# Four layers in one launch: one shared weight buffer whose next layer's weights are loaded before the layer before it ends, and the modulation's products made on DVE inside the second layer

## The reference, cut to what matters

```python
def first_block(x, positions, ...):
    for layer in range(DEPTH):                  # DEPTH = 2
        if layer % 2 == 0:
            x = _even_layer(x, *even_params[layer // 2])     # x @ w_in (3088 wide), gated linear attention, spatial gating
        else:
            x = _odd_layer(x, positions, *odd_params[layer // 2])   # x @ w_in (2560 wide), rotary, retention, pooling
    return x

def second_block(x, c, w_ada, b_ada, g_pre, w_in, ...):
    mod = jax.nn.silu(c) @ w_ada[layer] + b_ada[layer]       # [1024] @ [1024, 3072]
    shift, scale, gate = jnp.split(mod, 3, axis=-1)
    h = rmsnorm(x, g_pre[layer]) * (1.0 + scale[:, None, :]) + shift[:, None, :]
    proj = h @ w_in[layer]                                   # 3792 + 64 columns, split over the last two layers
    o_a = gated_deltanet(...)                                # third layer of the kernel
    o_b = dsa_sparse_attention(...)                          # fourth layer of the kernel
    mix = jnp.concatenate([o_a, o_b], axis=-1) @ w_out[layer]
    return x + gate[:, None, :] * rmsnorm(mix, g_post[layer])
```

## Time and profile before

| what | us |
|---|---|
| median of 3 runs (4527.81 to 4532.61) | 4531.23 |
| the profiled execution | 4529.71 |
| its span, first to last instruction | 4527.8 |
| PE busy | 4082.2 |
| DVE, ACT, POOL busy | 1905.7, 1396.9, 790.8 |
| mean granted clock of PE | 0.963 |

### The profile page before, as it was taken

One profiled execution on the slowest core, in us unless ns is written; L12 is line 12 of the kernel. 1 busy time (PEld: TensorE's weight loads), 2 busy tenths in 40 slices (PEclk: granted clock), 3 DMA queues, 4 the chain that ended last, 5 costly groups with the idle time before them and its releaser, 6 DMA issues. The chain is left out here.

```text
span 4527.8 us, 57307 instructions
## 1 busy us (share of the span) xinstructions
PE 4082.2 (90%) x23038; PEld 2629.7 (58%) x23038; DVE 1905.7 (42%) x4316; ACT 1396.9 (31%) x2956; POOL 790.8 (17%) x548
## 2 busy tenths in 40 slices
PE   7999999996799999996899999997789989898877
PEld 4555555553355555553688888886665656555544
DVE  0111111212122222222255555654046687688875
ACT  1222222222111111111133333332144445455552
POOL 1223323323022222221122222221000000000000
PEclk9999999998899999998999999996899999999998
DMA  5000000000400000003400000000310000000000
GB/s 180 19 14 14 19 19 9 19 19 10 168 19 19 19 19 19 19 19 104 154 23 25 25 25 25 20 15 6 136 33 33 22 29 17 31 20 17 17 12 17
DMA packets 73482, 161.03 MB, mean 36 GB/s; under 512 B 18053, under 2 KB 32058, under 8 KB 72250
## 3 DMA queue, kind: packets, MB, share of 16 engines
q1 hardware_dynamic: 73274, 158.14, 9.9%
HBM read 120.37 MB, written 37.75 MB: 35 GB/s over the span
## 5 line engine op out<-in xcount | busy, mean ns | idle before, releaser
L287 PE MATMUL e_ps<-e_w_in,e_xT 128*128 128x440 f32 (+1 forms) x1792 | 688.0, 538 | 1.8 <-DMA e_w_in<-l_w_in 1.8
L772 PE MATMUL o_ps<-o_w_in,o_xT 128*128 128x512 f32 x1280 | 565.0, 595 | 11.5 <-ACT o_xT L875 10.6
L287 PEld LDWEIGHTS e_ps<-e_w_in,e_xT 128*128 128x128 f32 x1792 | 332.9, 191 | 303.1 <-issue 295.8
L772 PEld LDWEIGHTS o_ps<-o_w_in,o_xT 128*128 128x128 f32 x1280 | 239.5, 191 | 290.9 <-issue 290.8
L1294 PE MATMUL d_ps<-d_hT,d_w_in 128*128 128x128 f32 x3072 | 392.9, 282 | 13.3 <-ACT d_hT L1485 11.3
L1294 PEld LDWEIGHTS d_ps<-d_hT,d_w_in 128*128 128x128 f32 x3072 | 360.0, 193 | 29.1 <-ACT d_hT L1485 12.7
L2096 PE MATMUL s_ps<-s_hT,s_w_in 128*128 128x128 f32 x2304 | 275.0, 280 | 8.1 <-DMA s_w_in<-w_in 5.6
L2096 PEld LDWEIGHTS s_ps<-s_hT,s_w_in 128*128 128x128 f32 x2304 | 270.9, 197 | 13.2 <-DMA s_w_in<-w_in 6.9
L856 PE MATMUL o_ps<-o_w_out,o_gt 128*128 128x512 f32 x512 | 225.2, 598 | 4.5 <-ACT o_gt L929 4.5
L2220 PE MATMUL s_ps<-s_w_out,s_catT 128*128 128x512 f32 x512 | 227.1, 597 | 0.0
L2238 PE MATMUL s_ps<-s_ikT,s_iqT 64*128 64x512 f32 (+3 forms) x608 | 168.5, 632 | 63.2 <-ACT s_Lg L2358 62.5
(11 more groups left out here) (408 smaller groups left out, 6106.6 us busy)
## 6 DMA issues: line engine op xcount, KB each, us to landing
d_ada<-w_ada SPq DMA_DIRECT2D x8, 1536.0 KB, 6.6
o_w_in<-l_w_in SPq DMA_DIRECT2D x5, 2048.0 KB, 17.8
e_xb<-x SPq DMA_DIRECT2D x16, 512.0 KB, 3.5
x<-e_gl SPq DMA_DIRECT2D x16, 512.0 KB, 2.6
o_xb<-x SPq DMA_DIRECT2D x16, 512.0 KB, 3.2
x<-o_cat SPq DMA_DIRECT2D x16, 512.0 KB, 2.6
d_xb<-x SPq DMA_DIRECT2D x16, 512.0 KB, 3.3
hT<-d_hT SPq DMA_DIRECT2D x16, 512.0 KB
```

The lines of the kernel that those rows point to most:

```text
L287: m = pe.matmul(bank[c % 2][:, 0:n], xT[:, k * P:(k + 1) * P], W_in[:, k, a:a + n], start=(k == 0), stop=(k == KT - 1))
L772: m = pe.matmul(bank[c % 2][:], xT[:, k * P:(k + 1) * P], W_in[:, k, off:off + 512], start=(k == 0), stop=(k == KT - 1))
```

## The change

One tile `arena` (128 partitions, 3088 columns by 8) is allocated once, and every layer's `W_in` is a view of its front. What lies behind a smaller `W_in` holds tables of that layer (`Carve`). `xb` (two blocks of x) and `ident` are shared too. A new class `Ahead` holds a layer's weight parts with their semaphores, so that the layer before it can issue the loads: SP does so as soon as the last block's projections are made (`proj_made.upto(BLOCKS - 1)`). The first two blocks of x, or for the last layer the first block of `hT`, are loaded ahead too. The small tables still load after the barrier.

Each layer's start is written in another order: weights ahead of tables in `even_layer`, PE's waits for `loaded` and `W_out` behind block 0's projections, the positions loaded as 16 rows and turned by PE. The product with `w_ada` leaves `delta_layer`. In each of the 16 blocks of `odd_layer` SP loads 192 columns of `w_ada` (8 rows of 768 bytes a partition, 0.79 MB), DVE multiplies them with `ccol` and adds up each partition's 8 rows, and SP stores the 128 x 192 sums to `mod_parts`. `delta_layer` loads `mod_parts` (1.57 MB) and adds the 128 partitions with six products with `ones`.

```diff
+class Ahead:
+    def __init__(self, sem, name, W_in, weights, parts, rows=None, xb=None):
...
+    def load_weights(self, eng):
+        for part, ready in zip(self.parts, self.w_loaded):
+            for dst, src in part:
+                eng.dma_start(dst, src).then_inc(ready.sem, 16)
+    def weights(self, n):
+        return self.w_loaded[n].sem, 16 * len(self.parts[n])
+    def load_rows(self, eng, n):
+        eng.dma_start(self.xb[:, n, :], self.rows[n * P:(n + 1) * P, :]).then_inc(self.x_in[n].sem, 16)
...
 # even_layer, SP
+            sp.dma_start(ident[:], ident_d).then_inc(ident_loaded.sem, 16)
+            own.load_rows(sp, 0)
+            own.load_weights(sp)
+            own.load_rows(sp, 1)
             with nc.allow_non_contiguous_dma(reason="small tables"):
...
             body(Blk(BLOCKS // 2 - 1, 0), load=False)
+            sp.wait_ge(stored.sem, 16 * (BLOCKS - 1) + 1)
+            ahead.load_rows(sp, 0)
+            sp.wait_ge(*proj_made.upto(BLOCKS - 1))
+            ahead.load_weights(sp)
+            sp.wait_ge(*r_ready.upto(BLOCKS - 1))
+            ahead.load_rows(sp, 1)
             body(Blk(BLOCKS // 2 - 1, 1), load=False)
...
 # odd_layer, SP
             def body(b, load=True):
+                sp.wait_ge(*ada_made.before(b.i))
+                sp.dma_start(ada, ada_v[:, :, bass.ds(b.i * ADA_N, ADA_N)]).then_inc(ada_in.sem, 16)
...
+                sp.wait_ge(*ada_made.upto(b.i))
+                sp.dma_start(mod_parts[:, bass.ds(b.i * ADA_N, ADA_N)], ada_sum[:]).then_inc(ada_stored.sem, 16)
                 sp.wait_ge(*out_ready.upto(b.i))
...
             body(Blk(BLOCKS // 2 - 1, 0), load=False)
+            sp.wait_ge(*proj_made.upto(BLOCKS - 1))
+            ahead.load_weights(sp)
             body(Blk(BLOCKS // 2 - 1, 1), load=False)
...
 # odd_layer, DVE, in each block
                 dve.tensor_tensor(cat[:, 0:512], cat[:, 0:512], gates[:, p, 0:512], ALU.mult).then_inc(*oc_ready.inc())
+                dve.wait_ge(ada_in.sem, 16 * i + 16)
+                dve.tensor_tensor(ada, ada, spread(ccol[:], ADA_N), ALU.mult).then_inc(*o.inc())
+                o.settle()
+                dve.wait_ge(ada_stored.sem, 16 * i + 1)
+                dve.tensor_reduce(ada_sum[:], ada.rearrange("p k n -> p n k"), AX.X, ALU.add).then_inc(*ada_made.inc())
                 dve.wait_ge(*y_made.upto(i))
...
 # delta_layer, SP and PE
-            for k in range(2, KT):
-                sp.wait_ge(ada_used.sem, k - 1)
-                load_ada(k)
-            for (a, n), part in zip(w_parts, w_loaded):
-                sp.dma_start(W_in[:, :, a:a + n], wv[:, :, a:a + n]).then_inc(part.sem, 16)
...
+                if b.i == BLOCKS - 2:
+                    sp.wait_ge(*proj_made.upto(BLOCKS - 1))
+                    sp.wait_ge(h_stored.sem, 16 * BLOCKS + 1)
+                    h_first.load(sp, 0)
+                    ahead.load_weights(sp)
...
-            pe.wait_ge(*c_ready.upto(0))
-            for k in range(KT):
-                pe.wait_ge(aloaded[k % 2].sem, 16 * (k // 2) + 16)
-                for n in range(6):
-                    m = pe.matmul(bank[n][:], cB[:, k, :], ada[:, k % 2, n * 512:(n + 1) * 512], start=(k == 0), stop=(k == KT - 1))
-                m.then_inc(*ada_used.inc())
+            pe.wait_ge(*ones_ready.upto(0))
+            pe.wait_ge(mod_loaded.sem, 16)
+            for n in (2, 3, 0, 1, 4, 5):
+                pe.matmul(bank[n][:], ones[:], mod[:, n * 512:(n + 1) * 512], start=True, stop=True).then_inc(*mod_made.inc())
...
 # sparse_layer, PE: block 0 waits for its weights alone, and the bias table is waited for behind block 1
+            for c in range(4):
+                pe.wait_ge(*own.weights(c))
+                project(0, c)
             pe.wait_ge(loaded.sem, NSMALL)
...
+            transpose_ckv(0)
             for c in range(4):
-                pe.wait_ge(w_loaded[c].sem, 16 * len(w_parts[c]))
-                project(0, c)
+                project(1, c)
+            pe.wait_ge(*cT_ready.upto(0))
             pe.wait_ge(loaded2.sem, 64)
```

338 lines of the change are left out of this document (179 added, 159 removed).

## The result

| | before | after |
|---|---|---|
| median of the runs, us | 4529.52 (4 runs, 4524.45 to 4532.61) | 4426.64 (4 runs, 4423.76 to 4429.24) |
| span of the profiled execution, us | 4527.8 | 4423.8 |
| PE / DVE busy, us | 4082.2 / 1905.7 | 4037.5 / 1977.8 |

The ratio is 0.9774, with a 95% interval of 0.9757 to 0.9791: 103 us faster, where the sum of the forecast was 92. The difference of the two profiled executions, 104.0 us, is read off at the same events in each. A start is counted from DVE's first instruction behind the barrier.

What follows compares the result with a forecast made beforehand. Blocks were taken as PE-bound, with layer starts waiting for loads; -9.0 - 27.9 - 45.8 - 9.5 = -92.2 us from 4529.7 gave 4437.5, stated as 4438 for the median; own range 4430 to 4447, wide range 4424 to 4453.

Steps and rivals of the forecast that it cites:

- three signs of being wrong: Idle PE ended by `conv_w` tables later than 2140, a sum over 4 us, or a wait for weights behind a barrier.
- More is gained: Rival: tables no limit at program start (-14 instead of -9), queue faster at other starts; -100, 4430 us; chance 0.08.
- first condition: At the program's start, tables are no limit, so that start gains 14 us instead of 9.
- Program start, -9.0: First layer's loop waits for tables but no longer for `W_out`, beginning at 53 instead of 62.07 us.
- Second layer, -27.9: Early weights and angles out of the way: first projection at 1133.1, loop at 1164.0 instead of 1191.93 us.
- Third layer, -47.8: `w_ada` product gone, `conv_w` tables late next: first projection at 2144.4 instead of 2192.25 us.
- The +1 for the lower clock in the projection: Third layer's first projection: PE, having stood idle longer, runs a first stretch at lower clock, costing 1 us.
- Tail of the second layer, +1: Block 15's `w_ada` share, queued behind 8.4 MB of weights, delays the end 1 us; 7 at 265 GB/s.
- The products cost nothing: Second layer's DVE product and sum, 3.6 us a block, hide in 17.9 us idle; sum priced 1.83, at most 3.7.
- Fourth layer, -9.5: Earlier first projection, partly lost to block 1's wait for `hT` behind the bias row; block 2 at 3247.7 instead of 3257.15.

Runs made afterwards that it cites:

- angles_first: Changed kernel with the second layer's old starting order restored: positions turned and sine, cosine made before x and the first projection; 4438.42 us.
- late_weights: Changed kernel with the early loads undone: each layer's x rows, turned h and weights issued at its own start; 4460.81 us.
- second pair: Kernel before and changed kernel, each executed and profiled once more without edits; 4534.62 us and 4429.08 us.
- product_back: Changed kernel with the `w_ada` product moved back to the third layer on PE, and its loads and DVE work removed from the second; 4470.15 us.
- tables_split: Changed kernel with the third layer's four `conv_w` loads on their own semaphore, awaited only before the first convolution; 4426.17 us.
- sum_5x: Changed kernel with DVE's sum over the eight row groups made five times a block in the second layer instead of once; 4444.09 us.
- sum_9x: Changed kernel with DVE's sum over the eight row groups made nine times a block in the second layer instead of once; 4590.3 us.
- h_ahead: Changed kernel with the fourth layer's second turned h issued ahead of the bias row's store and loads instead of behind them; 4421.10 us.

## Why the prediction was right

The mechanism came as the prediction has it, start by start, and none of its three signs of being wrong was seen: `conv_w` landed 21.5 us after the third layer's barrier (the sign was 2140, 26.8 us after it), the sum took 2.82 us, and no wait for weights stands behind a barrier. The size fits less well. The measured 4426.6 lies below the forecast's own range, 4430 to 4447, and within the wide one, 4424 to 4453; it is nearer to the time of the rival *More is gained* (4430) than to 4438. That rival's first condition did not come, as the tables still ended a wait at the program's start. Most of the difference lies in the third layer's last two blocks, which the sum left out.

- **Program start, -9.0, measured -12.2.** Mechanism right, the term mis-sized. The tables landed at 49.0 and not at 50.6, and behind them stood 1.7 us and not 2; with the 0.6 us that the 16 projection products next in line take less (7.91 against 8.52 us), the first two blocks shift by 12. No run undoes this part; it stands on the two traces.
- **Second layer, -27.9, measured -28.2.** Each step stands in the rows: first projection 2.8 us after the barrier (2.7 by the text's times), angles ready at 21.6 us (21.6). What I had not parted are the two causes: angles_first gives 13.2 to the order, late_weights 18.0 to the early loads. Against the second execution of the kernel before the gain is 26.0, so the nearness of the first is luck in part.
- **Third layer, -47.8 at its first projection, measured -47.2** (-49.0 in the second pair). The product is out of the way (product_back: 43.7 of it), and the tables of `conv_w` are late next, 21.5 us after the barrier (20.8 forecast); tables_split shows the row ahead of that, at 18.3. The +1 for the lower clock in the projection did not come: its row took 23.59 us, against 23.87. The six products, costed at 6.4 us, took 7.8; nothing waited for them.
- **Tail of the second layer, +1, measured +0.8.** The share landed at 2056.13, where the forecast, shifted by the 40.4 us gained until then, says 2056.3. The residual's 0.7 us came from the sum's own price, 2.78 us and not 1.83. The row itself proves little, as the same stretch of the kernel before took 912.48 and 913.33 us.
- **The products cost nothing: right.** 913.24 us with them, 913.00 without. The price of the sum was taken at the wrong end: 2.82 us lies in the middle between the 1.83 and the 3.7 of the text, 1.54 times the rate an element of the contiguous row. Here the cover hid it. sum_5x and sum_9x show that a price of 14 us would have been hidden in 15 blocks and paid in the last one.
- **Fourth layer, -9.5, measured -9.8.** The new wait for `hT` was forecast at some 8 us and was 9.16; h_ahead shows that most of it was no necessity. late_weights gave back 16.2 us here, more than was gained: the early loads are worth that much, and I take the 6 us between the two as the price of the bias row's new way, which h_ahead won back. The kernel before took 78.7 and 82.2 us in this stretch, so -9.5 was met with luck too.
- **What the sum left out**: -7.6 in the third layer's last two blocks. The text said that nothing behind a start changes, so the whole remainder shifts. The granted clock moves by itself there: the profiled execution of before had a long stretch, 94.1, and that of the changed kernel a short one. The repeat of before, 90.9, makes nearly half of it chance. The load of the fourth layer's weights is not needed for most of the rest, as late_weights has 88.2 without it. Whether the change has any other part in it stays open, as only two executions of before were profiled and one variant of the changed kernel, sum_5x, took 96.2. The fourth layer behind block 2 takes 1270 to 1277 us in the same way, not settled to a cause.
- The 11.8 us by which the profiled pair (104.0) exceeds the sum (92.2) are then 3.2 at the program's start, 8.6 in the third layer behind its first projection (-7.6 where the sum had +1), and nothing net over the rest.

## What to carry to other kernels

When a load moves ahead of a barrier, list what is late next and in which order it was issued: here the tables at the third layer and the bias row's way through DRAM at the fourth held their starts by 3 and 7 us more in the traces (the medians moved by 0.5 and 5.5 us). Idle time of an engine covers new work block by block; in block 15, where DVE waited 12 us for a queued transfer, none was left. Filling work to raise PE's clock can cost more than the clock gives back: 2 us at each place, longer than most of the waits, lost 15 us over two blocks; 0.5 us may have gained 4, by one execution. And before a forecast is called exact, execute the kernel before twice: here its own stretches moved by up to 3.5 us, one by 6.

## What was not expected of the hardware

- DVE's sum over eight elements 768 bytes apart takes 2.82 us for 1536 elements, 1.83 ns each, against 1.19 ns for contiguous ones (L1723 of the earlier trace rows). That row also makes 8 sums of 128 elements and this one 192 sums of 8; what is the distance's and what the short sums' part, no run tells.
- With unchanged instructions, PE's granted clock in a stretch full of short waits was 0.50 to 0.69 in its second half, and its length 86.9 to 96.2 us; in two executions of one program it agreed to 0.03 us, in two of another it differed by 3.2.
- A load of 512 KB landed 3.4 us after its issue when none was issued shortly before it, and 5.7 us behind four loads of 128 KB with 768 KB more issued behind it.
